# Attention of a hybrid encoder block written as 80 tile steps, with each step's share of the next head's projections between its values and its transposes

## What is computed

```
h = RMSNorm(x)
[qA|kA|vA|qB|kB|vB] = h @ w_in              # six times 512 columns
yA = neighbourhood attention, 8 heads of 64: softmax(qA kA^T / 8 + bias, masked to a window) vA, RMSNorm per head
yB = differential attention, 4 heads:  (softmax(q1 k1^T/8 + bias) - lam * softmax(q2 k2^T/8 + bias)) vB, RMSNorm per head
x = x + concat(yA, yB) @ w_out
x = x + ExpertChoiceMoE(RMSNorm(x))         # 16 SwiGLU experts, 2816 wide
final RMSNorm
```

## Time and profile before

| | |
|---|---|
| median of 3 runs | 3111.79 us (3108.22 to 3114.04) |
| the profiled execution, own time | 3127.45 us |
| its span, first to last instruction | 3125.8 us |
| PE, DVE, ACT, POOL busy | 92%, 63%, 55%, 30% |
| NA jobs, from the first score to the last projection | 145.7 to 505.1 us |
| projection of vB | 505.1 to 570.2 us |
| first three DF jobs | 570.2 to 841.3 us |
| last DF job | 841.3 to 915.4 us |

### The profile page before, as it was taken

One profiled execution on the slowest core, in us unless ns is written; L12 is line 12 of the kernel. 1 busy time (PEld: TensorE's weight loads), 2 busy tenths in 40 slices (PEclk: granted clock), 3 DMA queues, 4 the chain that ended last, 5 costly groups with the idle time before them and its releaser, 6 DMA issues.

```text
span 3125.8 us, 56149 instructions
## 1 busy us (share of the span) xinstructions
PE 2888.6 (92%) x23174; PEld 2660.1 (85%) x23174; DVE 1971.4 (63%) x2173; ACT 1731.7 (55%) x2603; POOL 925.1 (30%) x685
## 2 busy tenths in 40 slices
PE   4999999888879919999999999999999999999994
PEld 3977778777757719999999999999999999999994
DVE  4222221544443378778778788787787787787784
ACT  3144441443441117667667667677677676676673
POOL 2102221011121103334334344253253253353343
PEclk9999889998989959999999999999999999999997
DMA  6211101011113517888888887897898888888885
GB/s 168 81 27 34 32 24 48 1 35 34 56 63 135 216 43 268 301 312 283 300 318 277 309 311 275 312 321 267 310 326 286 311 301 287 308 301 301 296 292 203
DMA packets 351475, 654.41 MB, mean 209 GB/s; under 512 B 25175, under 2 KB 78551, under 8 KB 350743
## 3 DMA queue, kind: packets, MB, share of 16 engines
q1 hardware_dynamic: 339211, 606.41, 55.1%
q0 software_dynamic: 12048, 44.87, 5.0%
HBM read 615.82 MB, written 39.62 MB: 210 GB/s over the span
## 4 chain that ended last, share of the span: by engine, by line
PE 66%; DVE 3%; DMA 1%; issue 1%; POOL 1%; ACT 1%; SPq 0%; POOLq 0%; DVEq 0%; ACTq 0%
PE S L852 27%; PE OG L852 13%; PE S L855 13%; PE OG L855 6%; PE S L582 1%; PE S L584 1%; PE S L583 1%; PE PT L577 1%; DVE affT L1486 1%; PE OG L759 1%; DVE m L1484 1%; PE PT L824 1%; PE PT L827 0%; DVE E L1327 0%; PE PT L834 0%
## 5 line engine op out<-in xcount | busy, mean ns | idle before, releaser
L1542 DVE TENSOR_TENSOR wl<-stg,wh 128x2048 bf16<-128x2048 f32 (+1 forms) x544 | 1235.2, 2276 | 347.4 <-ACT wh L1153 347.3
L1153 ACT ACTIVATE wh<-stg 128x2048 fp32r<-128x2048 f32 (+1 forms) x544 | 1011.1, 1862 | 215.3 <-PE S L855 141.2
L1808 POOL TENSOR_TENSOR hx<-hh,hx 128x320 fp32r<-128x320 f32 x176 | 403.6, 2293 | 993.0 <-ACT hx L1197 993.0
L852 PE MATMUL S<-X,wh 128*128 128x320 f32 x3760 | 593.2, 313 | 1.2 <-DVE X L1547 1.2
L852 PEld LDWEIGHTS S<-X,wh 128*128 128x128 f32 x3760 | 556.7, 189 | 2.9 <-DVE X L1547 1.3
L852 PE MATMUL S<-hx,wh 128*128 128x320 f32 x1892 | 320.0, 315 | 0.0
L852 PE MATMUL OG<-X,wh 128*128 128x320 f32 x1872 | 298.9, 312 | 0.0
L855 PE MATMUL S<-Xb,wl 128*128 128x160 bf16 x3760 | 290.1, 233 | 0.0
L852 PEld LDWEIGHTS S<-hx,wh 128*128 128x128 f32 x1892 | 280.0, 188 | 0.9
L852 PEld LDWEIGHTS OG<-X,wh 128*128 128x128 f32 x1872 | 277.1, 188 | 0.8
L855 PEld LDWEIGHTS S<-Xb,wl 128*128 128x128 bf16 x3760 | 258.9, 98 | 12.0
(11 more groups left out here) (220 smaller groups left out, 4732.2 us busy)
## 6 DMA issues: line engine op xcount, KB each, us to landing
stg<-in_w_gate_dram SPq DMA_DIRECT2D x80, 2048.0 KB, 8.4
stg<-in_w_up_dram SPq DMA_DIRECT2D x80, 2048.0 KB, 10.9
stg<-in_w_down_dram SPq DMA_DIRECT2D x64, 2048.0 KB, 11.9
stg<-in_w_down_dram SPq DMA_DIRECT2D x32, 1536.0 KB, 10.5
stg<-in_w_gate_dram SPq DMA_DIRECT2D x16, 1024.0 KB, 5.4
stg<-in_w_up_dram SPq DMA_DIRECT2D x16, 1024.0 KB, 5.4
w_st<-in_w_in_dram SPq DMA_DIRECT2D x16, 512.0 KB
yt<-mixed SPq DMA_DIRECT2D x10, 512.0 KB, 3.8
```

The lines of the kernel that those rows point to most:

```text
L852: pe.matmul(out, w, x, start=first, stop=False, skip_group_check=True)
L1153: act.activation(piece_conv(wh, g), piece_stage(g), ACT.Copy).then_inc(rounded, 1)
L1542: dve.tensor_tensor(piece_conv(wl, g), piece_stage(g), piece_conv(wh, g).bitcast(F32), ALU.subtract).then_inc(split, 1)
L1808: pool.tensor_tensor(hx[:, f, CT:2 * CT], hh[:, :, :], hx[:, f, 0:CT].bitcast(F32), ALU.subtract).then_inc(hidden_ready, 1)
```

## The change

Attention is written out as 80 steps (`STEPS`), one for each job and tile, without loops. In a step of an NA job both heads are scored together. What each engine does in a step s is in the diff; in words:

- `scores(s)` issues each product for both halves (heads, or DF halves) in turn, on partitions 0 to 63 and 64 to 127, into the two halves of S. It waits until both maxima of step s-1 are read.
- then `values(s-2)`, for NA with the two heads' products alternating between the upper and the lower 64 output partitions. V is read in place; the copy `Vj` is gone.
- then, in one piece, the step's share of the projections of the next job: `SHARE` cuts a job's six chunks (`CHUNK`: k then q, each 512, 512 and 256 tokens) into ten shares. Chunks are built in one bank of OG, so k is double-buffered (`Kh`, `Kl`), and each chunk is rounded and written as soon as it is complete.
- then `turn_exps(s-1)` (for NA up to three fills of PT) and, for NA, the transpose of the output of step s-2, which now goes through a single bank.
- On DVE a step is `mix(s-1)` (DF), both `bias_max`, then `proj_lows` if a chunk is complete and `w_lows` on two steps of a job. On ACT it is `exps`, `df_out`/`oT_copy`, `exps`, `turned_copy(s-1)`, `proj_round`, `w_round`.
- Weights of q, k and vB now come in units of 128 columns through one staging buffer. vB is projected in three pieces of 128, 256 and 128 columns (`V_B`).
- The last DF head's normalisation and store are in three parts (tiles 0 to 3, 4 to 7, 8 and 9) where they were in two.

The core of the diff:

```
-            with pe.Fori(0, JOBS) as i:
...
-                for s in range(STEP):
-                    if s < UNITS:
...
-                        scores(n0 + s, s, s // 2, s % 2, kt0 * P, chunks)
-                    else:
...
-                        project(n0 + UNITS, s - UNITS)
-                    if 2 <= s < UNITS + 2:
...
-                        turn((f0, F_NA + NA_TURN[u]), list(range(na_blocks(u // 2))),
-                             lambda b: E[:, u % 4, b * P:(b + 1) * P])
-                    if 3 <= s < UNITS + 3:
...
-                        na_values(i, u // 2, u % 2, f0 + (F_NA + na_turned(u)), keys, kt0)
...
+CHUNK = [(1, 0, 512), (1, 512, 512), (1, NPR, NSA), (0, 0, 512), (0, 512, 512), (0, NPR, NSA)]
+SHARE = [(0, 0, 4), (0, 4, 8), (1, 0, 4), (1, 4, 8), (2, 0, 8), (3, 0, 4), (3, 4, 8), (4, 0, 4), (4, 4, 8), (5, 0, 8)]
...
+                for at_, key, ln in chunks:
+                    kk = slice(k0 + key, k0 + key + ln)
+                    for n, (a, b) in enumerate(((Qh, Kh), (Qh, Kl), (Ql, Kh))):
+                        for hf in range(2):
+                            rows = slice(64 * hf, 64 * hf + 64)
+                            mm = pe.matmul(S[:, hf, at_:at_ + ln], a[rows, q], b[j % 2][rows, kk],
+                                           start=(n == 0), stop=(n == 2))
...
+                    for b in range(nb):
+                        n = min(P, nk - b * P)
+                        for hf in range(2):
+                            mm = pe.matmul(O[64 * hf:64 * hf + 64, 0:P],
+                                           V[0:n, kt0 + b, cols.start + 64 * hf:cols.start + 64 * hf + 64],
+                                           PTs[0:n, hf * nb + b, :], start=(b == 0), stop=(b == nb - 1))
...
+            for s in range(NAS):
+                scores(s)
+                if s >= 2:
+                    values(s - 2)
+                project_part(s, 0)
+                project_part(s, 1)
+                if s >= 1:
+                    turn_exps(s - 1, (0, 1, 2))
+                if s >= 2:
+                    out_turn(s - 2)
...
+            for s in range(NAS, STEPS):
+                scores(s)
+                if s - 2 >= NAS:
+                    values(s - 2)
+                project_part(s, 0)
+                project_part(s, 1)
+                if s - 1 >= NAS:
+                    turn_exps(s - 1, (0, 1))
...
+            for s in range(NAS, STEPS):
+                j, t = s // TT, s % TT
+                exps(s, 0)
+                if s - 2 >= NAS:
+                    df_out(s - 2)
+                exps(s, 1)
+                if s - 1 >= NAS:
+                    turned_copy(s - 1)
+                step_project(s)
...
+            for s in range(NAS, STEPS):
+                j, t = s // TT, s % TT
+                if s - 1 >= NAS:
+                    mix(s - 1)
+                df_bias(s)
+                step_project(s)
...
+                if j == JOBS8 - 1 and t in (1, 3, 5, 7):
+                    wo_lows(t // 2)
```

More of the change, by code:

```diff
@@ L36 @@
 BIG = 3e38
[L39 to L41 removed]
+JOBS8 = 2 * JOBS
+NAS = JOBS * TT
+STEPS = JOBS8 * TT
+CHUNKS = 6
 def na_window(t):
@@ L109, with step_blocks, attention_fills @@
[L109 to L112, removed]
+def step_blocks(s):
+    return 2 * na_blocks(s % TT) if s < NAS else df_keys(s % TT)[1] // P
+def attention_fills():
+    n, turn, out = 2 * TT, {}, {}
+    for a, b in ((0, NAS), (NAS, STEPS)):
+        for s in range(a, b + 2):
+            if a <= s - 1 < b:
+                turn[s - 1] = n
+                n += -(-step_blocks(s - 1) // 4)
+            if b == NAS and s - 2 >= a:
+                out[s - 2] = n
+                n += 1
+    return turn, out, n
@@ L614, in scores, with project @@
-            def scores(n, u, t, hf, k0, chunks):
-                pe.wait_ge(scores_read, n - 1)
-                rows = slice(64 * hf, 64 * hf + 64)
+                mm.then_inc(v_ready, 1)
+            def project(j, c, k0, k1):
+                i, t0, ln = CHUNK[c]
+                if k0 == 0:
+                    pe.wait_ge(w_split, UNIT[j, i] + 1)
+                    if j:
+                        pe.wait_ge(fill_split, CHUNKS * j + c)
+                    elif c >= 2:
+                        pe.wait_ge(fill_split, c - 1)
+                out = OG[:, 1 if j else c % 2, 0:ln]
+                for k in range(k0, k1):
+                    mm = three(out, w_h[i][:, k, :], w_l[i][:, k, :], hT_h[:, k, t0:t0 + ln], hT_l[:, k, t0:t0 + ln],
+                               k == 0, k == KT - 1)
+                if k1 == KT:
+                    mm.then_inc(fill_ready, 1)
@@ new lines, in _ @@
+            pe.wait_ge(w_split, UNIT["v", 0] + 1)
+            values(NAS - 2)
+            v_tile(V_B, w_h[1], w_l[1], 0)
+            turn_exps(NAS - 1, (0,))
+            out_turn(NAS - 2)
+            v_tile(V_B + 1, w_h[1], w_l[1], 1)
+            values(NAS - 1)
+            v_tile(V_B + 2, w_h[1], w_l[1], 2)
+            out_turn(NAS - 1)
+            for t in range(3, TT):
+                v_tile(V_B + t, w_h[1], w_l[1], t)
+            pe.wait_ge(w_split, UNIT["v", 2] + 1)
+            for t in range(TT):
+                v_tile(V_B + TT + t, w2_h, w2_l, t)
```

943 lines of the change are left out of this document (456 added, 487 removed).

## The result

| | median | executions |
|---|---|---|
| kernel before | 3112.91 us | 4, from 3108.22 to 3117.20 |
| changed kernel | 3000.23 us | 4, from 2997.88 to 3003.18 |

The ratio is 0.9639, with a 95% interval from 0.9621 to 0.9656: 112.7 us less.

What follows compares the result with a forecast made beforehand. PE was taken to bound the NA jobs and lead the DF jobs. NA -74, vB +19, DF -42, last DF job +11, clock +12, end -3 give -77 us: 3050 (profiled) or 3035 (median); forecast 3045, range 3010 to 3100.

Steps and rivals of the forecast that it cites:

- NA jobs, 71.3 us each: Four NA jobs: each falls from 89.9 to 71.3 us, saving 74 us in all.
- values 160 x 0.109 = 17.4 us: NA jobs: 160 value products per job, each at the unpaired pace of 0.109 us, cost 17.4 us.
- the column halves pair: Rival, NA values: the two heads' products on different output partitions run at once, 26 us less, 3019 us; chance 25%.
- changes of kind 8: NA jobs: PE's switches between kinds of product, five a step at 0.16 us each, cost 8 us a job.
- Clock, +12 us: PE's clock: some 25 us still run at half speed, so 12 us are lost.
- I keep a quarter to a third of the old half-speed time: PE's clock: of about 65 us at half speed in the old NA jobs, some 25 us stay.
- DF jobs, 76.4 us each: First three DF jobs: each falls from 90.4 to 76.4 us, saving 42 us in all.
- 0.8 us for each of eight long steps: DF jobs: PE waits before `values` for ACT's copies, 6.4 us a job.
- DF steps queue: Rival, DF steps: the three engines take turns, a long step costs 10 us, not 8.3; 41 us more, 3085 us; 12%.
- vB, +19 us: vB stage: grows from 65.1 to 84 us, with 480 products of 128 columns at 0.109 us.
- The rival at the fp32 price: Rival, vB stage: 128-column products cost the fp32 price, 0.22 us; 50 us more, 3095 us; chance 17%.
- Last DF job, +11 us: Last DF job, with no projection: a pair of steps takes 18 us against 15.2, so four pairs lose 11 us.

Runs made afterwards that it cites:

- values apart: Changed kernel with the values of an NA tile issued head by head instead of alternating: 3024.77 us, ratio 0.9693 to the kernel before.
- the second profile: The kernel before, unchanged, profiled once more; the profiled execution took 3112.19 us, the first one 3127.45.
- bare jobs: Changed kernel with scores split around values, values head by head, and three in four projection products left out in NA jobs 1 and 2: 3105.05 us.
- mixed order: Changed kernel with, in DF steps only, a projection share that continues its chunk put before the values: 2993.90 us, ratio 0.9608.

## Why the prediction was right or wrong

What the change does was right, and so was every sign: projections beside `mix` and `bias_max`, scores in pairs, a longer vB, a longer last job. Three terms of the sum were wrong in size, and behind the first stands a mechanism that the forecast did not have. 3045 was 45 us too high; it had been put between the sum against the median (3035, 35 too high) and the sum against the profiled execution (3050, 47 too high).

*NA jobs, 71.3 us each.* **The step that failed most was "values 160 x 0.109 = 17.4 us".** What I had as a rival with a chance of 25%, "the column halves pair", is what happens: 0.0545 us each. The run with values apart puts an NA job at 72.4 us, 1.1 from my 71.3, with some of its pairs left, so the other terms of that sum (scores 6.6, shares 27.5, changes of kind 8) were right to a few us together; pairing takes it to 65.1. One reading behind them was wrong: what I gave as seen directly, 0.32 us against 0.23, is 0.09 for a change of kind and not 0.16. The 0.57 us a unit is borne out by the second profile, where a job's stretch at full clock takes 52.3 us (318.1 to 370.4), 11.9 over the content of 40.4, or 0.60 a unit. The four jobs take 258.3 us where the sum had 285.2, 27 less; the rival had priced the pairs at 26. I had given the rule a smaller chance for want of a row, and because its neighbour spoke against it. Of the two rules of the Trainium skill, TensorE: Matmul & The Clock Gate, "Part 3: Packing small matmuls", that on column groups holds here, with a factor of 2 for two; that weight loads need another row group to overlap would have kept values at 0.109, and the trace disagrees. The earlier trace rows spoke against it already: the weight loads of products over all 128 rows take 8.96 of 10.80 us there, under products that keep their 0.225.

*Clock, +12 us.* **The second step that failed was "I keep a quarter to a third of the old half-speed time".** (A third of the 65 us would be 22, not the 25 that I took; that is a small part.) Nothing of it is left in NA or vB, 1.00 in all; in the DF jobs two steps at 0.83 cost some 3 us. Pairing is not what does it (values apart: 1.00). The bare jobs say that the shares do (0.89 and 0.93 without most of them), but this is shown only so far: with a full share in each NA step every profile has 1.00, while without any the kernel before had 0.83 to 1.00 in its jobs, so shares are enough in NA jobs and not always needed. I had started from one execution with 18% of its NA time at half speed; the second has 6%. That also is where the 15.7 us lay which I could not place: 18.7 us of NA time. So the median of the kernel before held less lost time to win back than the sum counted with. At full clock a job of the kernel before, 52.3 us and a projection of 30.8, takes 83.1, four of them 332: of the 101 us that NA lost from profile to profile 27 are clock, and of the other 74 the pairs of values are 29.

*DF jobs, 76.4 us each.* They take 72.0, 73.0 and 70.0. **The third was "0.8 us for each of eight long steps" and the 2 us beside it, which was too much**: PE waits 13.8 us in three jobs, 4.6 a job in place of 8.4. `values` wait in 12 of 30 steps, in the others not at all. This is 11 of the 14 us by which the three jobs are shorter than the sum; the other 3 I cannot place. "DF steps queue" did not come: no `mix` in PE's waits.

*vB, +19 us.* It was 20.6. The narrow product's price was the one choice between far ends, and the lower end was right: 0.111 measured for 0.109 taken. The rival at the fp32 price is out.

*Last DF job, +11 us.* It was 7.4, and the chain has the links I had listed: 11.7 us for a step with a piece was 10.4 to 12.6, 6.3 for one without was 5.8. That moving one call would take 18 us off the stage I had not seen.

*Start and end.* Start 0, end -3: the wait for y, from PE's last value product to the first transpose of y, went from 8.7 only to 8.1 us. The start varied by chance from 142 to 151 us among executions of kernels with the same prologue.

Together: -27 (NA jobs), -12 (clock), -14 (DF jobs), +2 (vB), -4 (last job), +3 (end) and +5 (start, by chance) are -47, which is what profile against profile gives: 3003 - 3050. What stays open is why the kernel before runs the same stretch at 0.83 in one execution and at 1.00 in the next, and why in the changed kernel the DF jobs' ninth step fell to 0.83 in some jobs and not in others, and not at all in the mixed order.

## What to carry to other kernels

Issue small products so that halves of the array alternate, in rows or in columns, and test that pairing before costing it: alternating columns took 7 of 72 us off a job here. Spread the long products over the steps of a job: here it covered the waits for other engines, and PE's clock stood at 1.00 in the NA jobs, but a share that begins a new accumulation must stand behind other work as long as there is one accumulator bank. And look for a conversion that two engines do one after the other in a step's chain; letting the second lag a step was one moved call here and took 18 us off the stage.

## What the runs showed that I had not expected

- Products of the upper and of the lower 64 rows ran two at a time, 0.01 us apart, even when three of one half were issued before the three of the other; with full-height products between them they did not. The Trainium skill, TensorE: Matmul & The Clock Gate, "Part 3: Packing small matmuls", gives PE a reorder window for such loads, with which the trace agrees, and says that matmuls start strictly in order, with which it does not.
- Two column halves of full-height products ran at 0.0545 us each, alternating; issued head by head, sixteen took 1.58 us rather than 1.09, as only the ends of the two groups overlapped; eight took 0.66 us in either order.
- An operand read in two runs of 128 columns, 8 KB apart, costs 0.12 us at full clock, no more than one run of 256.
- The same kernel's NA jobs took 359.4 us at clock 0.91 in one execution and 340.7 at 0.97 in another. In twelve profiles of kernels with a share in every NA step, the jobs with full shares were at 1.00 in all.
